# Stick-breaking heads as items of the attention loop, memory keys in pieces between them, values item by item

## The reference

```
sp = where(causal, softplus(z), 0)
tail = cumsum(sp, reverse=True) - sp
a = where(causal, exp(log_sigmoid(z) - tail), 0)
```

## Time and profile before

| | us |
|---|---|
| median of 3 runs | 1877.91 (1877.75 to 1879.15) |
| the profiled execution | 1882.08, its span 1880.4 |
| PE busy | 1755.8 |
| DVE, ACT, POOL busy | 691.8, 701.2, 733.3 |
| mean granted clock of PE | 0.974 |
| layer 1: attention loop | 177.0 to 297.5 |
| layer 1: stick-breaking tail | 297.5 to 343.7 |
| layer 1: output projection | 343.7 to 387.3 |
| layer 1: memory keys | 387.3 to 411.4 |

### The profile page before, as it was taken

The page is one execution under the profiler, slowest core; times in us unless marked ns, Lnnn a source line. Parts: engine busy times, 40 slices in busy tenths (PEclk is TensorE's granted clock), DMA queues, the critical chain, the costliest instruction groups (busy, mean ns, idle before and its releaser), DMA issues.

```text
span 1880.4 us, 21420 instructions
## 1 busy us (share of the span) xinstructions
PE 1755.8 (93%) x8558; PEld 1388.9 (74%) x8558; DVE 691.8 (37%) x1470; ACT 701.2 (37%) x1284; POOL 733.3 (39%) x379
## 2 busy tenths in 40 slices
PE   6998899999988999999989978999999799999996
PEld 5887455788677888888778854558886688888885
DVE  3236773242424223221152468632314423242112
ACT  5215555353433222222352255554524422232231
POOL 4444320275233444444344443203841334444451
PEclk9998998999998999999989999999999899999998
DMA  4323100144122223223232321002431222322321
GB/s 160 111 74 111 46 2 1 56 136 145 55 69 68 90 93 109 90 90 105 77 112 90 95 68 46 1 1 79 166 115 34 78 79 95 107 90 92 104 84 56
DMA packets 100686, 154.03 MB, mean 82 GB/s; under 512 B 4284, under 2 KB 76268, under 8 KB 100588
## 3 DMA queue, kind: packets, MB, share of 16 engines
q1 hardware_dynamic: 97532, 147.16, 24.1%
q10 hardware_dynamic: 3056, 5.51, 0.9%
HBM read 150.56 MB, written 2.10 MB: 81 GB/s over the span
## 4 chain that ended last, share of the span: by engine, by line
PE 86%; DVE 7%; ACT 4%; issue 1%; POOL 1%; DMA 0%; ACTq 0%; DVEq 0%
PE banks L1236 23%; PE banks L1238 22%; PE banks L1237 22%; PE banks L1419 3%; PE banks L1437 2%; PE banks L1460 2%; PE banks L1256 1%; PE banks L1620 1%; DVE banks L974 1%; PE banks L1602 1%; DVE h L975 1%; PE banks L1508 1%; PE banks L1511 1%; ACT proj L754 1%; PE banks L1412 1%
## 5 line engine op out<-in xcount | busy, mean ns | idle before, releaser
L604 POOL TENSOR_TENSOR w_lo<-raw,w_hi 128x1024 fp32r<-128x1024 f32 (+1 forms) x280 | 672.0, 2421 | 949.6 <-ACT w_hi L668 949.6
L668 ACT ACTIVATE w_hi<-raw 128x1024 fp32r<-128x1024 f32 (+1 forms) x280 | 274.0, 1027 | 855.1 <-PE banks L1238 822.5
L1236 PE MATMUL banks<-w_hi,a_lo 128*128 128x512 f32 (+1 forms) x928 | 358.2, 386 | 1.4 <-ACT oT L743 1.4
L1238 PE MATMUL banks<-w_hi,a_hi 128*128 128x512 f32 (+1 forms) x928 | 355.7, 383 | 0.0
L1237 PE MATMUL banks<-w_lo,a_hi 128*128 128x512 f32 (+1 forms) x928 | 355.7, 383 | 0.0
L1236 PE MATMUL banks<-a_hi,w_lo 128*128 128x512 f32 x832 | 326.1, 392 | 0.0
L1237 PE MATMUL banks<-a_lo,w_hi 128*128 128x512 f32 x832 | 324.4, 390 | 0.0
L1238 PE MATMUL banks<-a_hi,w_hi 128*128 128x512 f32 x832 | 324.3, 390 | 0.0
L1236 PEld LDWEIGHTS banks<-w_hi,a_lo 128*128 128x128 f32 x928 | 174.9, 189 | 35.6 <-ACT oT L743 1.9
L1237 PEld LDWEIGHTS banks<-w_lo,a_hi 128*128 128x128 f32 x928 | 174.9, 188 | 34.0 <-issue 0.5
L1238 PEld LDWEIGHTS banks<-w_hi,a_hi 128*128 128x128 f32 x928 | 174.6, 188 | 33.6
(11 more groups left out here) (221 smaller groups left out, 2075.5 us busy)
## 6 DMA issues: line engine op xcount, KB each, us to landing
raw<-in_ffn_w_up SPq DMA_DIRECT2D x44, 1024.0 KB, 5.1
raw<-in_w_in SPq DMA_DIRECT2D x20, 1024.0 KB, 5.1
raw<-in_ffn_w_down SPq DMA_DIRECT2D x20, 1024.0 KB, 4.9
raw<-in_x_wk SPq DMA_DIRECT2D x8, 1024.0 KB, 5.3
raw<-in_x_wv SPq DMA_DIRECT2D x8, 1024.0 KB, 4.9
raw<-in_x_wq SPq DMA_DIRECT2D x8, 1024.0 KB, 5.3
raw<-in_x_wo SPq DMA_DIRECT2D x8, 1024.0 KB, 4.9
raw<-in_cmp_wk SPq DMA_DIRECT2D x4, 1024.0 KB, 5.3
```

What stands on the lines that cost most here:

```text
L604: inc(pool.tensor_tensor(w_lo[:, u % RING, n * half:n * half + n], raw[:, u % RING, n * half:n * half + n], w_hi[:, u % RING, n * half:n * ...
L668: inc(act.activation(w_hi[:, u % RING, first:first + n_half], raw[:, u % RING, first:first + n_half], ACT.Copy), hi_made)
L1236: pe.matmul(dst, st_lo, mv_hi, start=first, stop=False)
L1238: return pe.matmul(dst, st_hi, mv_hi, start=False, stop=last)
```

## The change

The stick-breaking pairs 6 and 7 become groups `sb` of four items in the list, like the softmax groups: query rows on partitions, keys along the row. Item i of kind sb goes so: PE's `scores(i)`; DVE adds the strict mask and copies to SBUF (`zcopied`); POOL makes max(z,0) (`stick_relu`); ACT makes ln(1+exp(-|z|)) in three passes; DVE makes the suffix sum of both with `tensor_tensor_scan`, on a reversed row, one for each head; POOL subtracts it from z (`stick_log`); PE transposes; ACT takes the exponential while it copies out of both banks; PE multiplies the values. The tail, its triangles and their constants go.

The values of every kind are made by item: t+1 key tiles by 128 query columns for each head half. The output gathers in bank 6 alone, so the first value of a pair waits for `oT_done` of the pair before. Transposes lag 3 steps, values 4. All softmax scales are POOL's, both halves, except the items ahead of a low half, which are DVE's. NI is 52.

The units of the memory keys come ahead of the output's. Their products run in 16 pieces of 12 matmuls (`keys_of_memory`) at the steps in `FILL_STEPS`, in bank 7, and ACT copies them (`xk_copy`). ACT casts six weight units in the loop (CAST_STEPS). m_hi and m_lo are made in steps 0 to 7; `o_parts` run in the loop. After the last scores PE makes the first four banks of output unit 0 in the last four steps (`out_unit_0`), and the memory values then use banks 0 to 3 right after the output projection.

```diff
-U_IN, U_CMP, U_OUT, U_XK, U_XV, U_XQ, U_XO, U_UP, U_DOWN = 0, 12, 16, 20, 24, 28, 32, 36, 58
+U_IN, U_CMP, U_XK, U_OUT, U_XV, U_XQ, U_XO, U_UP, U_DOWN = 0, 12, 16, 20, 24, 28, 32, 36, 58
-GROUPS = [(m, "moba") for m in range(2)] + [(m, k) for m in range(2, 6) for k in ("sel", "cmp", "win")]
+GROUPS = [(0, "moba"), (1, "moba"), (6, "sb"), (2, "sel"), (2, "cmp"), (2, "win"), (3, "sel"), (3, "cmp"), (3, "win"),
+          (7, "sb"), (4, "sel"), (4, "cmp"), (4, "win"), (5, "sel"), (5, "cmp"), (5, "win")]
-LAG_SCALE, LAG_T, LAG_V = 1, 2, 3
+LAG_T, LAG_V = 3, 4
+FILL_STEPS = [9, 9, 10, 10, 11, 11, 12, 13, 31, 31, 32, 32, 33, 33, 34, 35]
+CAST_STEPS = {2: 1, 5: 2, 15: 3, 19: 4, 38: 5, 43: 6}
+LO_STEPS = {3: (0, 0), 4: (0, 1), 6: (1, 0), 7: (1, 1), 16: (2, 0), 18: (2, 1), 20: (3, 0), 22: (3, 1),
+            39: (4, 0), 41: (4, 1), 44: (5, 0), 46: (5, 1)}
+BY_DVE = [i for i in range(NI) if i + 1 in LO_STEPS and SOFT[i]]
+O_STEPS = {14: 0, 41: 1}
...
+                def stick_relu(i):
+                    pool.wait_ge(zcopied.sem, zcopied.at(l, sb_at(i)))
+                    if sb_at(i) > 2:
+                        pool.wait_ge(scanned.sem, scanned.at(l, sb_at(i) - 2))
+                    inc(pool.tensor_scalar(rb(i), zb(i), 3.0e38, 0.0, ALU.min, ALU.max), relued)
+                def stick_log(i):
+                    pool.wait_ge(scanned.sem, scanned.at(l, sb_at(i)))
+                    inc(pool.tensor_tensor(both(i), zb(i), both(i), ALU.subtract), sb_d)
...
+                        link(act.activation(both(i), zb(i), ACT.Abs))
+                        link(act.activation(both(i), both(i), ACT.Exp, scale=-1.0))
+                        inc(act.activation(both(i), both(i), ACT.Ln, bias=1.0), sb_l)
...
                 for i in range(STEPS + 1):
+                    for n in range(8):
+                        if FILL_STEPS[2 * n + 1] == i - 1:
+                            xk_copy(n)
                     if i < NI:
                         exponentials(i)
+                    if i < KD:
+                        mem_hi(i)
+                    if i in CAST_STEPS:
+                        cast_to(U_XK + CAST_STEPS[i])
                     if 0 <= i - LAG_T < NI:
                         copy_T(i - LAG_T)
+                    if i in O_STEPS:
+                        act.wait_ge(qk.sem, qk.at(l, i))
+                        o_parts(O_STEPS[i])
+                    for m in range(8):
+                        last = LAST[max(g for g in range(len(GROUPS)) if GROUPS[g][0] == m)]
+                        if last == i - 1 - LAG_V:
+                            copy_o(m, pv, last + 1)
...
+                        for hp in range(2):
+                            p = probs(i, hp)
+                            ins = dve.tensor_tensor_scan(p[:, ::-1], rb(i)[:, hp, ::-1], p[:, ::-1], 0.0, ALU.add, ALU.add)
+                        inc(ins, scanned)
...
+                def values(i):
+                    g, t = ITEMS[i]
                     m, kind = GROUPS[g]
+                    pe.wait_ge(copied_act.sem, copied_act.at(l, i + 1))
+                    if SOFT[i]:
+                        pe.wait_ge(copied_dve.sem, copied_dve.at(l, soft_before(i + 1)))
+                    if kind in ("moba", "sel", "sb") and t == 0 and OT_ORDER.index(m):
+                        pe.wait_ge(oT_done.sem, oT_done.at(l, OT_ORDER.index(m)))
+                    for k in range(T if kind == "cmp" else t + 1):
+                        for kg in range(2):
+                            half = slice(HD * kg, HD * kg + HD)
...
+                                ins = pe.matmul(bank(6, P, P * t)[half], proj[:, k, col:col + HD], pT(i)[:, kg, P * k:P * k + P],
+                                                start=kind != "win" and t == 0 and k == 0, stop=kind != "sel" and k == t, skip_group_check=True)
+                    inc(ins, pv)
...
                 for i in range(STEPS):
                     if i < NI:
                         scores(i)
+                    for q in range(16):
+                        if FILL_STEPS[q] == i:
+                            keys_of_memory(q)
+                    if i >= NI:
+                        out_unit_0(i - NI)
                     if LAG_T <= i < NI + LAG_T:
                         transposes(i - LAG_T)
+                    if i >= LAG_V:
+                        values(i - LAG_V)
                     if i in CMP_STEPS:
                         compressed(CMP_STEPS.index(i))
```

More of the change, by code:

```diff
@@ L78, with upto, per_half, psums @@
 XSTEPS = max(XPIECES) + 1
[L79 to L86, removed]
+def upto(kinds, i):
+    return sum(k in kinds for k in KIND[:i])
 def item_keys(i):
     return P * (ITEMS[i][1] + 1)
[L94 to L101, removed]
+def per_half(i, hp):
+    return 2 * upto(("moba", "sel", "win"), i) + upto(("cmp",), i) + hp + 1
+def psums(i, hp):
+    return 2 * i - upto(("cmp",), i) + hp + 1
+def soft_before(i):
+    return sum(SOFT[:i])
+def sb_at(i):
+    return upto(("sb",), i) + 1
 def dve_scaled(i):
-    return sum(1 if CMP[j] else 1 + (j in BY_DVE) for j in range(i + 1))
-def pool_scaled(i):
-    return sum(not CMP[j] and j not in BY_DVE for j in range(i + 1))
+    return sum(KIND[j] == "cmp" or 2 * (j in BY_DVE) for j in range(i + 1))
+def pool_scaled(i, hp):
+    return sum(2 * (SOFT[j] and j not in BY_DVE) for j in range(i)) + hp + 1
 def blk_bank(b):
@@ L389, in unit_source @@
                 return ffn_w_down[l].rearrange("(k p) n -> p k n", p=P)[:, k[0]:k[-1] + 1, :]
-            for w, first, last in ((w_out, U_OUT, U_XK), (x_wv, U_XV, U_XQ), (x_wo, U_XO, U_UP)):
+            for w, first, last in ((w_out, U_OUT, U_XV), (x_wv, U_XV, U_XQ), (x_wo, U_XO, U_UP)):
                 if first <= u < last:
@@ L393, in unit_source @@
                     return w[l].rearrange("(k p) n -> p k n", p=P)[:, k:k + 2, :]
-            for w, first, last in ((x_wk, U_XK, U_XV), (x_wq, U_XQ, U_XO)):
+            for w, first, last in ((x_wk, U_XK, U_OUT), (x_wq, U_XQ, U_XO)):
                 if first <= u < last:
@@ L768, in copy_T @@
[L768 to L777 removed]
+                    m = GROUPS[ITEMS[i][0]][0]
@@ new lines, in values, with keys_of_memory @@
+                    inc(ins, pv)
+                def keys_of_memory(q):
+                    u, m, half = q // 4, q // 2 % 2, q % 2
+                    hi, lo = unit(U_XK + u)
+                    if half:
+                        rest(U_XK + u)
+                    if q == 0:
+                        pe.wait_ge(mT_lo.sem, mT_lo.at(l, KD))
+                        pe.wait_ge(vc_ready.sem, vc_ready.at(l, 1))
+                    if q % 2 == 0 and q:
+                        pe.wait_ge(xk_ready.sem, xk_ready.at(l, q // 2))
+                    for k in range(4 * half, 4 * half + 4):
+                        mm = slice(P * m, P * m + P)
+                        ins = three(bank(7, MEM, MEM * m), hi[:, k, mm], lo[:, k, mm], m_hi[:, k, :], m_lo[:, k, :], k == 0, k == KD - 1)
+                    if half:
+                        inc(ins, (xk_psum, unit_used)[m])
@@ new lines, in out_unit_0 @@
+                def out_unit_0(b):
+                    hi, lo = unit(U_OUT)
+                    rest(U_OUT)
+                    pe.wait_ge(o_lo.sem, o_lo.at(l, 1))
+                    pe.wait_ge(exped.sem, exped.at(l, n_half))
+                    t, n = divmod(b, 2)
+                    st = slice(P * t, P * t + P)
+                    for k in range(2):
+                        three(bank(b), a_hi[:, k, st], a_lo[:, k, st], hi[:, k, 512 * n:512 * n + 512], lo[:, k, 512 * n:512 * n + 512], k == 0, False)
```

465 lines of the change are left out of this document (184 added, 281 removed).

## The result

The changed kernel took 1908.62 us (median of 4 runs, 1907.33 to 1909.63), the kernel before 1877.83 (4 runs, 1876.79 to 1879.15): ratio 1.0164, 95% interval 1.0148 to 1.018. It is 31 us slower; the prediction was 18 us faster. The profiled execution took 1908.76 us.

A forecast was written before the change was run, and what follows sets the result against it. TensorE, busy 93% of the span, was taken as the bound. New loop 181.6 against 190.8 us gains 9.2 a layer, 18.4 in all: 1882.1 - 18.4 = 1863.7, set to 1860 as the profiled run lay above the median; range 1820 to 1888.

The forecast's parts named there:

- Removed work: Per layer, the stick-breaking tail (46.2 us) and the memory keys' stage (24.1 us) go.
- rival D: Around the output product: covers only exchanged, keys no longer hide the norm chain, values late; about 1877 us, chance 0.08.
- PE work: TensorE's work in the new loop, values by item, stick-breaking items and key pieces included: 148.6 us a layer.
- rival B: Weight loads of the values: 0.52 us a pair instead of 0.25, deciding from 0.33; 1924 us, chance 0.08.
- Waits: TensorE's waits in the new loop, from casts, output bank, first steps and others: 33 us a layer.
- bank waits: First values of a head pair wait for ScalarE's copy out of bank 6: seven times, 13.1 us a layer.
- cast waits: Six ScalarE weight casts stand ahead of the transposed copy; TensorE waits 9.0 us a layer, step 38 not counted.
- Rival A: Queue waits in the loop don't add up, staying at 12.5 us a layer; 1818 us, chance 0.22.
- the term: GpSimd and VectorE in each other's way during low passes in the loop: 3.3 us more waits a layer.
- The scan: VectorE's suffix sum in the stick-breaking chain: between 0.6 twice and 2.2 us, hidden behind the memory key pieces.
- Rival C: GpSimd's low passes each delay VectorE's copy and the transposes, 20 us a layer instead of 3.3; 1893 us, chance 0.12.
- New loop 148.6+33 = 181.6: One layer's loop as TensorE work plus waits, in us, a gain of 9.2 us a layer.

The follow-up runs named there:

- e6: The changed kernel with all softmax scales on GpSimd, none on VectorE beside GpSimd's low halves; 1905.4 us.
- e3: The changed kernel with 116 unused dummy matmuls of 128x256 a layer in steps where TensorE waits; 1905.0 us.
- e12: The changed kernel with 60 unused dummy matmuls of 128x128 a layer in the waits of steps 1 to 4; 1908.75 us.
- e4: The changed kernel with the 116 dummy matmuls a layer of e3, each one step later, where TensorE hardly waits; 1936.1 us.
- e2: The changed kernel with the output of head pairs 2 and 4 gathered in bank 7 instead of bank 6; 1892.2 us.
- e7: The changed kernel with five of sixteen key pieces moved into steps with waits (16, 20, 25, 38, 38); 1882.3 us.
- e14: e7 plus e6, with VectorE's memory low parts one step later, the last key piece at step 43 and that step's cast at 45; 1872.05 us.
- e1: The changed kernel with ScalarE's loop casts of weight units behind its copies in the step, not ahead; 1904.5 us.
- e10: e7 with VectorE's memory low parts one step later and the casts of steps 38 and 43 at 36 and 41; 1892.35 us.
- e8: The changed kernel with memory-token parts and two casts moved from steps 0-7 to 8-15, first eight key pieces and two casts later; 1912.0 us.
- e5: The changed kernel with e1 and e2 together; 1891.4 us.

## Why the prediction was wrong

Point by point, by its own steps.

- Removed work, output unit 0, output product, values of memory: right. Less than 1 us is lost outside the loop, so rival D is out.
- PE work: right at the full clock, 149.3 us for 147.3. Value pairs cost 0.257 us for 0.25, so rival B (from 0.33) is out as a property of the loads. The 0.53 seen behind waits is the clock's.
- Waits: 36.2 for 33. The bank waits sum to 11.9 for 13.1; the one at step 16 (counted in full at 1.7) was 0.66, because the cast of step 15 had already spent 2.42 there, where 0.4 had been forecast: the compressed scores don't cover a cast. The cast waits of steps 2, 5, 19 and 43 were 3.39, 1.32, 1.79 and 2.61 for 3.0, 2.1, 1.6 and 1.9. Rival A is out: it put them at 12.5 in all.
- GpSimd and VectorE: the lock is real, 4.12 us for two scales (so the trace agrees with the Trainium skill's "SBUF — State Buffer", section "SBUF: two separate sides", named in the prediction), but PE waited 3.3 us for VectorE's copies, as the term said; e6 gave 3 us in two layers. The scan of 512 columns took 1.37 us for a half on the mean, 2.7 a pair, above the upper bound of 2.2; it stayed hidden. Rival C is out.
- **The step that failed** is the sum "New loop 148.6+33 = 181.6". It took PE's work at the durations of the old loop and only added the waits to it. PE's busy time came out at 173.5 for 154.1, at a granted clock of 0.85 for 0.94; 17.4 of these 19.4 us are work at the low level. The old loop has 12.5 us of waits in 120.5, the new one 36.2 in 209.7, and the clock falls in them or behind them. The rows for this were there: the old kernel's loop had clocks of 0.94 and 0.97 in its two layers with 12.5 and 13.8 us of waits, and its key stage, almost without gaps, 1.00. They give a sign and no firm price (the higher clock of the two loops stands beside the longer waits), but a bound was due. (1 - 0.94) x 120.5 is 7.2 us beside 12.5 of waits, (1 - 0.97) x 120.8 is 3.6 beside 13.8. At these rates 33 us of waits cost 9 to 19 us, of which the old durations hold 7.2: 2 to 12 more a layer (an estimate). That alone takes the gain of 9.2 a layer to between +8 and -3, and it is still short of the 17.4 that came.

What is shown: work put into waits is free and raises the clock (e3, e12), the same work one step later costs 27.5 us (e4), and waits removed give back time in busy PE as well (e2, e7, e14). What is not: how much clock a given wait costs. By the loops above it ran from less than nothing (e1: 5.3 us of waits less, 2.5 more busy) to about the wait's own length (e2), and e7 and e10 differ by 8.5 us of busy time at equal waits. Nor is it shown what the compressed scores cost, behind which the clock fell without a wait; no kernel here changed them. e14 still waits 23 us a layer, 8.5 of them up to step 8, and e8 shows 12.6 us in layer 1 to be had there if the extra work found a better place than the stick-breaking steps. No kernel here found one.

## What to carry to other kernels

When a change adds waits to TensorE, price them at up to twice their length (in the loops of layer 1 here the low level cost 0.6 to 0.85 us for each us of wait). Read the clock in the windows of the kernel before against the waits in them: 0.94 with a tenth of waits was the warning. Then find each stretch at 0.50 and look at what stood ahead of it, a wait or a group of tiny matmuls. Where a busy time is off, take the time at the low level out of it first: here that left 2 us of error in the work. Filler work belongs in the steps where TensorE waits, not in those where it fits the data's order: five numbers in a list were worth 26 us. And before a queue's order is blamed for a wait, ask what is next in that queue: moving the cast (e1, e5, e10) only handed the wait on.

## What the runs showed of the hardware

- Behind a wait of 2.42 us TensorE's groups took 1.6 to 2 times their usual time for some 5 us, at work for which they waited for nothing; with dummy matmuls in place of the waits of steps 1 to 4 the stretch from 188 to 213 us rose from a granted clock of 0.70 to 0.79.
- In the change's first loop the granted clock was 0.50 for 61.4 of 209.7 us, in eight stretches, each begun inside a wait or at most 0.4 us behind one. Three of the five falls in the old kernel's loops (259.33, 283.23, 1184.35) came behind groups of 32-column matmuls, 11 to 12 us after the last wait.
- Equal sums of waits (27.2 and 27.7 us) went with clocks of 0.89 and 0.86 and 8.5 us of difference; the slower of the two also scattered over 11 us in six runs, the other over 2 in ten, and the kernel before over 12 in the 13 runs beside the latter.
- VectorE's scale of 128x384 took 2.06 us beside a GpSimd pass, one of 128x512 took 0.49 without one. VectorE's scans took 0.59, 0.96, 1.34 and 1.37 us on the mean for 128, 256, 384 and 512 columns. A GpSimd pass ran beside part of each pair, so these means give no price per column.
